# Packed half tiles in four feed-forward blocks, and a closing norm spread over more attention items, with its root taken by logarithm and exponential

## The chip, the cores and the metric

The kernel runs on one core of one Trainium2 chip, in one launch. The metric is the time of that launch on the device, in microseconds (us). The engines are TensorE (PE, whose weight loads are shown as PEld), VectorE (DVE), ScalarE (ACT), GpSimd (POOL) and SyncE (SP, which issues most loads).

## The reference

Two stacks of two layers each follow one another on 256 positions of width 1024, in float32.

The first stack works on 272 positions (16 meta positions ahead of the 256). Each layer is a SwiGLU block, a mixer (pooling, convolution, retention) and a second SwiGLU block, each closed by a residual layer norm:

```python
D_FF = ((8 * D_MODEL // 3 + 63) // 64) * 64        # 2752 = 21.5 tiles of 128

def swiglu_ffn(x, w13, w2):
    a, u = jnp.split(x @ w13, 2, axis=-1)
    return (jax.nn.silu(a) * u) @ w2
```

So there are four such blocks, and their hidden width is 21 tiles of 128 and one half tile of 64. The second stack is a diffusion-style transformer. Its first layer has a mixer of two parts, neighbourhood attention (8 heads of 64) and a bidirectional mLSTM (4 heads of 128), and the mLSTM's output is closed per head:

```python
def _mlstm_output(h, o_pre, g):
    h = sigmoid(o_pre) * h
    mu = jnp.mean(h, axis=-1, keepdims=True)
    var = jnp.mean(jnp.square(h - mu), axis=-1, keepdims=True)
    h = (h - mu) * lax.rsqrt(var + EPS)
    return h * g
```

Both parts go side by side through one output projection.

## The kernel before

All activations are kept feature-major: 128 features on the partitions, positions along the free axis. Each float32 weight is split into a high part, rounded to fp32r, and the rest, and so is each activation. A product of the two is three matmuls into the same PSUM tile: high by high, high by low, low by high (`three`, all of them recorded at line 448, where `mm` stands).

**Weights.** They come in units of 1 MB, a tile of 128 partitions by 2048 floats, each 16 blocks of 128 by 128. SP loads them in order into four slots (`load_unit`, L462). A load waits until the matmuls that read the slot's last unit are done. ACT makes the high part (`high`, L1430), DVE the rest (`rest`, L1975), and `w1_split` tells PE that a unit is ready.

**A feed-forward block of the first stack** (`ffn1`) has 33 units: 22 up units (f = 0 to 21), each with one tile of the gate and one of the value, 48 matmuls in all, and 11 down units (d = 0 to 10), two hidden tiles each, also 48 matmuls. The half tile (f = 21) is padded with zeros to a whole one in both. For each f, ACT takes the silu of the gate's tile from PSUM (L1487), DVE multiplies the value's tile on it (`gate`, L2118), ACT rounds it (`gate_high`, L1491), and DVE takes the rest (`gate_low`, L2122). DVE's program has the order `gate(step - 1)`, `rest` of the unit two ahead, some operations of the modulation's product (`ada_ops`, L2003 and L2006), `gate_low(step - 1)`. How many of those operations a step takes is said by `ada_due`: 3 in most up steps, 2 in every fourth, 4 in nine of the down steps, 96 in all. After steps 10, 15 and 21 DVE takes a finished part of the modulation from PSUM bank 7 (`ada_take`, L2011). The down product begins with the eight output tiles in the order 6, 2, 3, 4, 5, 7, 0, 1 (bank j holds tile j); tile 7 waits for that `ada_take`, tile 0 for the last `gate`. The last two down units are done tile by tile, so that tiles are finished one after another. Six DVE additions and the norm follow.

**The attention of the second stack's first layer** runs 32 items (`attend` on PE and DVE, `softmax` on ACT), items 0 to 15 over 256 keys and 16 to 31 over 512. For item n PE's program has the scores of n + 2 (and a bias product from item 16 on), the transposes of n (L1188), the values of n - 1, and then `between(n)`. DVE has the row maximum, the sum's reciprocal, the scaling of the probabilities, the placing of the output, and `between(n)`; ACT the exponential, two copies, and `between(n)`. `between` is where the mLSTM's closing norm is fitted in, by `head_norm(n - HEAD_SHIFT)`, with `HEAD_SHIFT` 14:

- items 12 to 15: for each head a mean by a product with ones (PE), the centring (DVE, L2504), the square (ACT, L1793)
- item 16: the variances of all four heads, into 32 partitions each (PE); item 17: the square root (ACT, L1796, into the tile `HSTD`); item 18: its reciprocal (DVE, L2507)
- items 18 to 21: for each head a product that spreads the reciprocals over all partitions (PE); items 19 to 22 the gain (DVE, L2511); items 20 to 24 the rounding and the rest (ACT L1799, DVE L2516)

The squares and `HSTD` lie in the weights' fourth slot, so SP waits for the last of those spreading products (`head_mm`) before it loads the unit `E_WOUT + 3`, one of the output projection's.

Of the kernel before, what the change touches and what calls it, by code (L numbers as in the profile page):

```python
# [71 lines left out]
def build(nc, A, out):  # L72
    with ExitStack() as ctx:
# [214 lines left out]
        GATES_OUT, CUM_OUT, NF_OUT = 1, 2, 3  # L288
        WG_SPLIT, GATES_ABS, LS_MIN, LS_DONE, CUM_COPIED, ROWS_COPIED, NF_COPIED = 1, 4, 5, 6, 7, 8, 9
        WG_HIGH, GATES_EXP, GATES_LN = 1, 2, 3  # L290
        HEAD_VAR, HEAD_STD = 5, 5
        HEAD_SHIFT = 14
        OG_TAKEN, VM_TAKEN = 6, 8
        OD_DQ, OD_CK, OD_KPE, OD_QR = 1, 2, 3, 4

# [11 lines left out]
        def conv_at(i, f):  # L307
            return 8 + FT * i + f + 1

        HEAD_CENTRED, HEAD_RSTD = (1, 2, 3, 4), 5  # L310
        HEAD_Y, HEAD_LOW = (6, 7, 8, 10), (9, 11, 12, 13)


        w1_loaded = [sem(f"w1_loaded{s}") for s in range(SLOTS)]
# [105 lines left out]

        ADA_FROM = [0]
# [246 lines left out]
        def _(pe):  # L668
# [5 lines left out]
            def three(o, n, b, hi, lo, first, last):  # L674
# [81 lines left out]
            def ffn1(l, b):  # L756
# [34 lines left out]
                for j in range(CT):  # L791
                    for d in range(DN_EARLY, DN_UNITS):
                        for kk in range(2):
                            k = 2 * d + kk
                            last = three(PS[:, j, tk], u0 + FT + d, kk * CT + j, GHI[:, k, tk], GLO[:, k, tk], False,
                                         k == FT - 1)
# [345 lines left out]
            def head_norm(n):  # L1142


                if n in (-2, -1, 0, 1):
                    h = n + 2
                    if h < 2:
                        pe.wait_ge(na_taken, NA_TILES)
                    else:
                        pe.wait_ge(head_step, HEAD_CENTRED[h - 2])  # L1150
                    pe.wait_ge(ml_out, h + 1)
                    mm(pe, PS[:, h % 2, :], ONES[:, 2, :], G[:, 8 + h, :], True, True).then_inc(head_mm, 1)
                elif n == 2:
                    pe.wait_ge(head_step, HEAD_CENTRED[3])
                    pe.wait_ge(pool2_step, ROW_SET)
                    for h in range(MLH):
                        pe.wait_ge(head_act, h + 1)
                        last = mm(pe, PS[32 * h:32 * h + 32, 0, :], ONES[:, 2, 0:32], OSQ2[:, h, :], True, True)
                    last.then_inc(head_mm, 1)
                elif n in (4, 5, 6, 7):  # L1160
                    h = n - 4
                    pe.wait_ge(head_step, HEAD_RSTD)
                    if h >= 2:
                        pe.wait_ge(head_step, HEAD_Y[h - 2])
                    mm(pe, PS[:, (h + 1) % 2, :], ROW2[32 * h:32 * h + 1, :], HSTD[32 * h:32 * h + 1, :], True, True)\
                        .then_inc(head_mm, 1)
# [250 lines left out]
        def _(act):  # L1417
# [3 lines left out]
            def high(n):  # L1421
# [8 lines left out]
                act.copy(WHI1[:, s, :], RAW[:, s, :]).then_inc(w1_high, 1)  # L1430

            def norm_out(e, gain, bias):
                tk = tokens(e - 1)
# [43 lines left out]
            def ffn1(l, b):  # L1477
# [4 lines left out]
                def silu(f):  # L1482
                    n, value = released[u0 + f]
                    act.wait_ge(n, value)
                    if FT * i + f >= 2:
                        act.wait_ge(g_low, FT * i + f - 1)
                    act.activation(SG[:, f % 2, tk], PS[:, 2 * (f % 3), tk], ACT.Silu).then_inc(silu1_done, 1)  # L1487

                def gate_high(f):
                    act.wait_ge(gated, FT * i + f + 1)  # L1490
                    act.copy(GHI[:, f, tk], SG[:, f % 2, tk]).then_inc(g_high, 1)  # L1491

                high(u0 + 2)
                high(u0 + 3)
# [292 lines left out]

            def head_norm(n):

                if n in (0, 1, 2):  # L1790
                    for h in ((0, 1), (2,), (3,))[n]:
                        act.wait_ge(head_step, HEAD_CENTRED[h])
                        act.activation(OSQ2[:, h, :], G[:, 8 + h, :], ACT.Square).then_inc(head_act, 1)  # L1793
                elif n == 3:
                    act.wait_ge(head_mm, HEAD_VAR)
                    act.activation(HSTD[:, :], PS[:, 0, :], ACT.Sqrt, bias=EPS6[:, 0:1]).then_inc(head_act, 1)  # L1796
                elif n in (6, 7, 8, 9):
                    act.wait_ge(head_step, HEAD_Y[n - 6])
                    act.copy(XB[:, :, 0, 4 + n - 6, :], two(G[:, 8 + n - 6, :])).then_inc(head_act, 1)  # L1799

            def softmax(items, base, probs, turned, banks, between):
                def copy_turned(n):
# [163 lines left out]
        def _(v):  # L1966
            v.memset(MODF[:, :, :], 0.0).then_inc(start_set, 1)

            def rest(n):

                if n >= UNITS:
                    return
                s = slot_of[n]
                v.wait_ge(w1_high, highs[n])
                v.tensor_tensor(WLO1[:, s, :], RAW[:, s, :], WHI1[:, s, :].bitcast(F32), ALU.subtract)\  # L1975
                    .then_inc(w1_split, 1)

            gst = Steps(v, gains_step)
# [131 lines left out]
            def ffn1(l, b):  # L2110
# [3 lines left out]

                def gate(f):
                    v.wait_ge(silu1_done, FT * i + f + 1)
                    t = SG[:, f % 2, tk]
                    v.tensor_tensor(t, t, PS[:, 2 * (f % 3) + 1, tk], ALU.mult).then_inc(gated, 1)  # L2118

                def gate_low(f):  # L2120
                    v.wait_ge(g_high, FT * i + f + 1)
                    v.tensor_tensor(GLO[:, f, tk], SG[:, f % 2, tk], GHI[:, f, tk].bitcast(F32), ALU.subtract)\  # L2122
                        .then_inc(g_low, 1)

                rest(u0 + 2)
# [372 lines left out]

            def head_norm(n):

                if n in (-2, -1, 0, 1):
                    h = n + 2
# [5 lines left out]
                if 5 <= n < 5 + MLH:  # L2508
                    h = n - 5
# [3 lines left out]
                if 7 <= n < 7 + MLH:  # L2513
                    h = n - 7
# [183 lines left out]
def up_units(w):  # L2698

    h = w.shape[1] // 2  # L2700
    w = np.pad(w.reshape(D, 2, h), ((0, 0), (0, 0), (0, FF - h)))
    return w.reshape(CT, P, 2, FT, P).transpose(3, 1, 2, 0, 4).reshape(FT, P, 2 * D)


def down_pairs(w):

    w = np.pad(w, ((0, FF - w.shape[0]), (0, 0)))
    return w.reshape(DN_UNITS, 2, P, CT, P).transpose(0, 2, 1, 3, 4).reshape(DN_UNITS, P, 2 * D)


# [137 lines left out]
```

## Time and profile before

| | |
|---|---|
| median of 3 runs | 2326.58 us (2322.51 to 2329.9) |
| the profiled execution | 2322.65 us, its span 2320.9 us |
| PE busy in the span | 2216.4 us (96%) |
| PEld | 2030.0 us (87%) |
| DVE | 1611.2 us (69%) |
| ACT | 1046.7 us (45%) |
| POOL | 209.8 us (9%) |
| mean granted TensorE clock | 0.969 |
| HBM | 330.5 MB read, 143 GB/s |

The profile is that of one execution. Its own time is 3.9 us under the median and equal to the fastest of the three runs. A matmul's duration in it is longer than the time that it adds, since matmuls overlap: what one costs is read from the start of one to the start of the next, or from the number of them in a stretch that PE fills. A bracket at the end of a timeline's line gives the idle time of the engine just ahead of it and whom it waited for.

### The profile page before, as it was taken

The page shows a single profiled execution, that of the slowest core. Times are in us where ns is not written, and L with a number is a line of the kernel's source. Part 1 is how long each engine was busy: PE and PEld are TensorE (multiplying, and loading weights), DVE is VectorE, ACT ScalarE, POOL GpSimd, SP SyncE. Part 2 cuts the span into 40 slices and gives each one's busy share as a digit, 9 for nine tenths or more (in the row PEclk, how much of TensorE's full clock was granted, in tenths as well). Part 3 has the DMA queues.
Part 4 walks back from the last instruction along what each step waited for, and adds up shares of the span by engine and source line. Part 5 has one row for each costly group of instructions (what it writes and reads, how often), then busy time and mean ns, then how long its engine had stood idle before and what let it go on. Part 6 is the DMA issues. An engine that isn't in the chain of part 4 may idle for free. (4 is left out here: it accounts for less than half of the span.)

```text
span 2320.9 us, 35981 instructions
## 1 busy us (share of the span) xinstructions
PE 2216.4 (96%) x15136; PEld 2030.0 (87%) x15136; DVE 1611.2 (69%) x2407; ACT 1046.7 (45%) x1512; POOL 209.8 (9%) x219
## 2 busy tenths in 40 slices
PE   6999998999999999899999998999999997997997
PEld 6999978999999997899999776698888886687997
DVE  5878886877887789697853467666455437757774
ACT  5433535433544344444444335534444323755662
POOL 2100232100210023210100001000000000100000
PEclk9999989999999999999998999999999998998998
DMA  5665524667466552476522112022322222113552
GB/s 212 241 218 204 193 73 152 241 224 255 182 220 218 199 193 85 186 256 236 201 91 79 55 55 79 19 73 91 105 95 91 104 78 74 54 42 115 186 177 100
DMA packets 47488, 333.86 MB, mean 144 GB/s; under 512 B 5532, under 2 KB 6652, under 8 KB 7776
## 3 DMA queue, kind: packets, MB, share of 16 engines
q1 hardware_dynamic: 37808, 268.45, 32.3%
q0 software_dynamic: 9520, 63.11, 7.3%
q8 instruction: 120, 1.97, 0.3%
q14 instruction: 40, 0.33, 0.0%
HBM read 330.50 MB, written 1.05 MB: 143 GB/s over the span
## 5 line engine op out<-in xcount | busy, mean ns | idle before, releaser
L1975 DVE TENSOR_TENSOR WLO<-RAW,WHI 128x2048 fp32r<-128x2048 f32 x252 | 587.9, 2335 | 269.4 <-ACT WHI L1430 266.6
L448 PE MATMUL PS<-XB,WHI 128*128 128x256 f32 (+1 forms) x3072 | 701.0, 323 | 15.5 <-DVE XB L2320 10.7
L1430 ACT CAST WHI<-RAW 128x2048 fp32r<-128x2048 f32 x252 | 479.8, 1907 | 317.8 <-DMA RAW<-in_dn_c 79.8
L448 PEld LDWEIGHTS PS<-XB,WHI 128*128 128x128 f32 x3072 | 517.4, 192 | 62.8 <-issue 18.1
L448 PE MATMUL PS<-XHI,WHI 128*128 128x272 f32 (+1 forms) x1792 | 523.3, 295 | 18.3 <-ACT XHI L1438 14.9
L448 PE MATMUL PS<-XHI,WLO 128*128 128x272 f32 (+1 forms) x1792 | 518.1, 292 | 0.0
L448 PE MATMUL PS<-XLO,WHI 128*128 128x272 f32 (+1 forms) x1792 | 495.2, 290 | 0.0
L448 PE MATMUL PS<-XB,WLO 128*128 128x256 f32 (+1 forms) x1536 | 494.0, 322 | 0.0
L448 PEld LDWEIGHTS PS<-XHI,WHI 128*128 128x128 f32 x1792 | 346.3, 193 | 23.8 <-issue 18.8
L448 PEld LDWEIGHTS PS<-XHI,WLO 128*128 128x128 f32 x1792 | 345.8, 193 | 0.0
L448 PEld LDWEIGHTS PS<-XLO,WHI 128*128 128x128 f32 x1792 | 334.1, 192 | 0.4
L448 PEld LDWEIGHTS PS<-XB,WLO 128*128 128x128 f32 x1536 | 294.9, 192 | 21.1
L2006 DVE SCALAR_TENSOR_TENSOR AP<-AW,SC,AP 128x512 f32<-128x512 f32 x336 | 241.5, 770 | 0.0
L448 PE MATMUL PS<-GHI,WLO 128*128 128x272 f32 (+1 forms) x704 | 201.3, 286 | 0.0
L448 PE MATMUL PS<-GHI,WHI 128*128 128x272 f32 (+1 forms) x704 | 201.2, 286 | 0.0
L448 PE MATMUL PS<-GLO,WHI 128*128 128x272 f32 (+1 forms) x704 | 201.0, 285 | 0.0
L2364 DVE SCALAR_TENSOR_TENSOR AC<-CB,FCW,AC 128x512 f32<-128x512 f32 (+1 forms) x176 | 97.1, 614 | 134.0 <-ACT AC L1658 103.8
L1487 ACT ACTIVATE SG<-PS 128x272 f32<-128x272 f32 (+1 forms) x88 | 34.2, 394 | 224.4 <-PE PS L448 224.4
L448 PEld LDWEIGHTS PS<-GHI,WHI 128*128 128x128 f32 x704 | 132.5, 188 | 0.0
L448 PEld LDWEIGHTS PS<-GHI,WLO 128*128 128x128 f32 x704 | 132.4, 188 | 0.0
L448 PEld LDWEIGHTS PS<-GLO,WHI 128*128 128x128 f32 x704 | 132.4, 188 | 0.0
L1656 ACT COPY CB<-PS 128x512 f32<-128x512 f32 x52 | 27.9, 589 | 114.0 <-PE PS L448 114.0
(362 smaller groups left out, 2735.1 us busy)
## 6 DMA issues: line engine op xcount, KB each, us to landing
AW<-in_ada POOLq DMA_DIRECT2D x48, 1024.0 KB, 6.7
RAW<-in_up_a SPq DMA_DIRECT2D x44, 1024.0 KB, 4.9
RAW<-in_up_b SPq DMA_DIRECT2D x44, 1024.0 KB, 4.9
RAW<-in_up_c SPq DMA_DIRECT2D x44, 1024.0 KB, 4.9
RAW<-in_mix SPq DMA_DIRECT2D x30, 1024.0 KB, 4.9
RAW<-in_dn_a SPq DMA_DIRECT2D x22, 1024.0 KB, 4.9
RAW<-in_dn_b SPq DMA_DIRECT2D x22, 1024.0 KB, 4.9
RAW<-in_dn_c SPq DMA_DIRECT2D x22, 1024.0 KB, 4.8
```

The costliest lines, as they stand in the source:

```text
L448: return pe.matmul(o, w, x, start=first, stop=last)
L1430: act.copy(WHI1[:, s, :], RAW[:, s, :]).then_inc(w1_high, 1)
L1487: act.activation(SG[:, f % 2, tk], PS[:, 2 * (f % 3), tk], ACT.Silu).then_inc(silu1_done, 1)
L1656: act.copy(cb[:, a, :, 1:257], two(PS[:, banks + a, :]))
L1975: v.tensor_tensor(WLO1[:, s, :], RAW[:, s, :], WHI1[:, s, :].bitcast(F32), ALU.subtract)\
L2006: v.scalar_tensor_tensor(a, w, c, a, ALU.mult, ALU.add).then_inc(ada_step, 1)
L2364: return v.scalar_tensor_tensor(o, i, vec(a, t), o, ALU.mult, ALU.add)
```

## The change

1. **Half tiles, up product.** The last up unit of each of the four blocks holds 64 columns of the gate and 64 of the value in one tile. It is 1024 floats wide: half of it is loaded, rounded and split, and PE does 24 matmuls in place of 48. Silu reads the lower 64 partitions, `gate` the upper 64 as the other operand.
2. **Half tiles, down product.** The hidden tile 21 holds its high part on the lower 64 partitions and its low part on the upper 64; the weights' rows are there twice. Two matmuls over 128 rows (`stacked`) take the place of three, eight output tiles in each block.
3. **`ada_due`**: the last up step takes no modulation operations in place of 3, steps 3 and 7 take 3 in place of 2, the sum stays 96.
4. **The closing norm** runs from item 10 to item 28: means at items 10, 11, 13, 14, each centring one item later and each square two; variances at item 18; at item 19 a logarithm, at item 20 an exponential of minus half of it (both ACT) in place of the square root and the reciprocal; spreading products at items 21, 22, 24, 25, the gain one item later, the rounding two, the rest three.

```diff
-        HEAD_VAR, HEAD_STD = 5, 5
-        HEAD_SHIFT = 14
+        HEAD_VAR, HEAD_LN, HEAD_STD = 5, 5, 6
+        HEAD_SHIFT = 10
+        MEAN_AT, SPREAD_AT = (0, 1, 3, 4), (11, 12, 14, 15)
...
+        HALF_UNITS = tuple(u + FT - 1 for u in (0, UNITS_B0, UNITS_LAYER, UNITS_LAYER + UNITS_B0))
+
+        def width(n):
+
+            return D if n in HALF_UNITS else 2 * D
+
+        def rows_of(f, a=0):
+
+            return slice(0, P) if f < FT - 1 else slice(64 * a, 64 * a + 64)
...
-                return 2 if step % 4 == 3 else 3 if step < FT else 0
+                return 0 if step == FT - 1 else 2 if step in (11, 15, 19) else 3
...
-                sp.dma_start(RAW[:, slot_of[n], :], src).then_inc(w1_loaded[slot_of[n]], 16)
+                w = width(n)
+                sp.dma_start(RAW[:, slot_of[n], 0:w], src[:, 0:w]).then_inc(w1_loaded[slot_of[n]], 16)
...
+            def stacked(o, n, b, hl, first, last):
+
+
+                wh, wl = block_of(n, b)
+                mm(pe, o, wh, hl, first, False)
+                return mm(pe, o, wl, hl, False, last)
...
-                for j in range(2):
+                for j in range(width(n) // D):
...
+                            if k == FT - 1:
+                                last = stacked(PS[:, j, tk], u0 + FT + d, kk * CT + j, GHI[:, k, tk], False, True)
...
-                elif n == 2:
+                elif n == 8:
...
-                elif n in (4, 5, 6, 7):
-                    h = n - 4
-                    pe.wait_ge(head_step, HEAD_RSTD)
+                elif n in SPREAD_AT:
+                    h = SPREAD_AT.index(n)
+                    pe.wait_ge(head_act, HEAD_STD)
...
-                elif n == 3:
+                if n == 9:
                     act.wait_ge(head_mm, HEAD_VAR)
-                    act.activation(HSTD[:, :], PS[:, 0, :], ACT.Sqrt, bias=EPS6[:, 0:1]).then_inc(head_act, 1)
+                    act.activation(HSTD[:, :], PS[:, 0, :], ACT.Ln, bias=EPS6[:, 0:1]).then_inc(head_act, 1)
+                if n == 10:
+                    act.wait_ge(head_act, HEAD_LN)
+                    act.activation(HSTD[:, :], HSTD[:, :], ACT.Exp, scale=-0.5).then_inc(head_act, 1)
...
-                    t = SG[:, f % 2, tk]
-                    v.tensor_tensor(t, t, PS[:, 2 * (f % 3) + 1, tk], ALU.mult).then_inc(gated, 1)
+                    t = SG[rows_of(f), f % 2, tk]
+                    u = PS[rows_of(f, 1), 2 * (f % 3) + (f < FT - 1), tk]
+                    v.tensor_tensor(t, t, u, ALU.mult).then_inc(gated, 1)
...
+                    r = rows_of(f)
+                    o = GLO[:, f, tk] if f < FT - 1 else GHI[rows_of(f, 1), f, tk]
+                    v.tensor_tensor(o, SG[r, f % 2, tk], GHI[r, f, tk].bitcast(F32), ALU.subtract)\
...
-                if n in (-2, -1, 0, 1):
-                    h = n + 2
+                if n - 1 in MEAN_AT:
+                    h = MEAN_AT.index(n - 1)
...
-                if n == 4:
-                    v.wait_ge(head_act, HEAD_STD)
-                    v.reciprocal(HSTD[:, :], HSTD[:, :]).then_inc(head_step, 1)
```

## Rows read from the trace of the kernel before

**Rows 1.** The page, part 1: busy time of each engine.

```profile
PE 2216.4 (96%) x15136; PEld 2030.0 (87%) x15136; DVE 1611.2 (69%) x2407; ACT 1046.7 (45%) x1512; POOL 209.8 (9%) x219
```

**Rows 2.** Windows: us, busy PE, PEld, DVE, ACT, POOL, granted clock, DMA share, GB/s.

```profile
42.00:170.00 128.00, 127.89 (x1016) 127.51 (x1015) 105.34 (x124) 51.88 (x63) 12.72 (x12) 1.00 0.64 230
977.00:1097.00 120.00, 119.65 (x1011) 119.35 (x1010) 103.56 (x134) 51.15 (x62) 12.21 (x12) 1.00 0.71 255
```

**Rows 3.** Timeline of ACT, end of the first block's up half.

```profile
170.45 0.40 ACT L1487 ACTIVATE SG<-PS 128x272 f32<-128x272 f32 x1 [3.55 <-PE PS L448]
171.27 1.91 ACT L1430 CAST WHI<-RAW 128x2048 fp32r<-128x2048 f32 x1 [0.42 <-DMA RAW<-in_dn_a]
```

**Rows 4.** Timeline of DVE, the same place.

```profile
166.62 2.29 DVE L1975 TENSOR_TENSOR WLO<-RAW,WHI 128x2048 fp32r<-128x2048 f32 x1 [1.36 <-ACT WHI L1430]
168.83 2.07 DVE L2006 SCALAR_TENSOR_TENSOR AP<-AW,SC,AP 128x512 f32<-128x512 f32 x3
170.82 0.43 DVE L2122 TENSOR_TENSOR GLO<-SG,GHI 128x272 fp32r<-128x272 f32 x1
171.17 0.16 DVE L2011 TENSOR_TENSOR MOD<-PS,ADAB 128x8 f32<-128x8 f32 x1
```

**Rows 5.** Timeline of ACT, fourth feed-forward block.

```profile
1017.95 0.38 ACT L1487 ACTIVATE SG<-PS 128x256 f32<-128x256 f32 x1
...
1097.13 0.39 ACT L1487 ACTIVATE SG<-PS 128x256 f32<-128x256 f32 x1 [3.20 <-PE PS L448]
```

**Rows 6.** Timeline of DVE, fourth feed-forward block.

```profile
1013.19 2.28 DVE L1975 TENSOR_TENSOR WLO<-RAW,WHI 128x2048 fp32r<-128x2048 f32 x1
...
1093.66 2.29 DVE L1975 TENSOR_TENSOR WLO<-RAW,WHI 128x2048 fp32r<-128x2048 f32 x1 [1.38 <-ACT WHI L1430]
```

**Rows 7.** Timeline of PE, the first attention.

```profile
1431.14 0.44 PE L1188 MATMUL PS<-IDN,PR 128*128 128x128 f32 x2 [0.32 <-DVE PR L2534]
...
1434.08 0.44 PE L1188 MATMUL PS<-IDN,PR 128*128 128x128 f32 x2 [0.32 <-DVE PR L2534]
...
1437.07 0.44 PE L1188 MATMUL PS<-IDN,PR 128*128 128x128 f32 x2 [0.81 <-DVE PR L2534]
...
1437.79 1.02 PE L448 MATMUL PS<-G,ONES 128*128 128x512 f32 x2
1438.65 1.02 PE L448 MATMUL PS<-G,QZ 128*128 128x512 f32 x2
...
1451.96 1.10 PE L448 MATMUL PS<-G,QZ 128*128 128x512 f32 x2 [0.89 <-ACT PR L1821]
...
1457.91 1.12 PE L448 MATMUL PS<-HSTD,ROW 1*128 1x512 f32 x2 [3.09 <-DVE HSTD L2507]
...
1465.90 0.60 PE L1188 MATMUL PS<-IDN,PR 128*128 128x128 f32 x4
...
1469.77 0.60 PE L1188 MATMUL PS<-IDN,PR 128*128 128x128 f32 x4
...
1482.11 0.60 PE L1188 MATMUL PS<-IDN,PR 128*128 128x128 f32 x4
...
1484.74 0.60 PE L1188 MATMUL PS<-IDN,PR 128*128 128x128 f32 x4
```

**Rows 8.** Timeline of ACT, the square root in the attention.

```profile
1447.75 1.28 ACT L1796 ACT_TABLE_LOAD   x1
...
1449.75 1.28 ACT L1821 ACT_TABLE_LOAD   x1
```

**Rows 9.** Timeline of DVE, the reciprocal of the roots.

```profile
1454.53 3.33 DVE L2507 RECIPROCAL HSTD<-HSTD 128x512 f32<-128x512 f32 x1
```

**Rows 10.** Window behind that wait, columns as in rows 2.

```profile
1458.00:1462.50 4.50, 4.50 (x11) 2.42 (x12) 0.97 (x2) 0.00 (x0) 0.00 (x0) 0.62 0.00 0
```

**Rows 11.** Timeline of ACT, table loads around the gates' logarithm.

```profile
1265.23 1.28 ACT L1734 ACT_TABLE_LOAD   x1
...
1304.45 1.28 ACT L1775 ACT_TABLE_LOAD   x1
```

More of the change, by code:

```diff
@@ L308, in conv_at @@
             return 8 + FT * i + f + 1
-        HEAD_CENTRED, HEAD_RSTD = (1, 2, 3, 4), 5
-        HEAD_Y, HEAD_LOW = (6, 7, 8, 10), (9, 11, 12, 13)
+        HEAD_CENTRED = (1, 2, 3, 4)
+        HEAD_Y, HEAD_LOW = (5, 6, 8, 10), (7, 9, 11, 12)
         w1_loaded = [sem(f"w1_loaded{s}") for s in range(SLOTS)]
@@ L794, in ffn1 @@
                             k = 2 * d + kk
-                            last = three(PS[:, j, tk], u0 + FT + d, kk * CT + j, GHI[:, k, tk], GLO[:, k, tk], False,
-                                         k == FT - 1)
+                            if k == FT - 1:
+                                last = stacked(PS[:, j, tk], u0 + FT + d, kk * CT + j, GHI[:, k, tk], False, True)
+                            else:
+                                last = three(PS[:, j, tk], u0 + FT + d, kk * CT + j, GHI[:, k, tk], GLO[:, k, tk],
+                                             False, False)
                     last.then_inc(tile_out, 1)
@@ L1142, in head_norm @@
             def head_norm(n):
-                if n in (-2, -1, 0, 1):
-                    h = n + 2
+                if n in MEAN_AT:
+                    h = MEAN_AT.index(n)
                     if h < 2:
@@ L1429, in high @@
                     act.wait_ge(r, value)
-                act.copy(WHI1[:, s, :], RAW[:, s, :]).then_inc(w1_high, 1)
+                w = width(n)
+                act.copy(WHI1[:, s, 0:w], RAW[:, s, 0:w]).then_inc(w1_high, 1)
             def norm_out(e, gain, bias):
@@ L1486, in silu @@
                         act.wait_ge(g_low, FT * i + f - 1)
-                    act.activation(SG[:, f % 2, tk], PS[:, 2 * (f % 3), tk], ACT.Silu).then_inc(silu1_done, 1)
+                    r = rows_of(f)
+                    act.activation(SG[r, f % 2, tk], PS[r, 2 * (f % 3), tk], ACT.Silu).then_inc(silu1_done, 1)
                 def gate_high(f):
                     act.wait_ge(gated, FT * i + f + 1)
-                    act.copy(GHI[:, f, tk], SG[:, f % 2, tk]).then_inc(g_high, 1)
+                    r = rows_of(f)
+                    act.copy(GHI[r, f, tk], SG[r, f % 2, tk]).then_inc(g_high, 1)
                 high(u0 + 2)
@@ L1788, in head_norm @@
             def head_norm(n):
[L1790 to L1793, printed above, removed]
-                elif n == 3:
-                    act.wait_ge(head_mm, HEAD_VAR)
-                    act.activation(HSTD[:, :], PS[:, 0, :], ACT.Sqrt, bias=EPS6[:, 0:1]).then_inc(head_act, 1)
-                elif n in (6, 7, 8, 9):
-                    act.wait_ge(head_step, HEAD_Y[n - 6])
-                    act.copy(XB[:, :, 0, 4 + n - 6, :], two(G[:, 8 + n - 6, :])).then_inc(head_act, 1)
+                if n - 2 in MEAN_AT:
+                    h = MEAN_AT.index(n - 2)
+                    act.wait_ge(head_step, HEAD_CENTRED[h])
+                    act.activation(OSQ2[:, h, :], G[:, 8 + h, :], ACT.Square).then_inc(head_act, 1)
+                if n == 9:
+                    act.wait_ge(head_mm, HEAD_VAR)
+                    act.activation(HSTD[:, :], PS[:, 0, :], ACT.Ln, bias=EPS6[:, 0:1]).then_inc(head_act, 1)
+                if n == 10:
+                    act.wait_ge(head_act, HEAD_LN)
+                    act.activation(HSTD[:, :], HSTD[:, :], ACT.Exp, scale=-0.5).then_inc(head_act, 1)
+                if n - 2 in SPREAD_AT:
+                    h = SPREAD_AT.index(n - 2)
+                    act.wait_ge(head_step, HEAD_Y[h])
+                    act.copy(XB[:, :, 0, 4 + h, :], two(G[:, 8 + h, :])).then_inc(head_act, 1)
             def softmax(items, base, probs, turned, banks, between):
@@ L1974, in rest @@
                 v.wait_ge(w1_high, highs[n])
-                v.tensor_tensor(WLO1[:, s, :], RAW[:, s, :], WHI1[:, s, :].bitcast(F32), ALU.subtract)\
+                w = width(n)
+                v.tensor_tensor(WLO1[:, s, 0:w], RAW[:, s, 0:w], WHI1[:, s, 0:w].bitcast(F32), ALU.subtract)\
                     .then_inc(w1_split, 1)
@@ L2499, in head_norm @@
             def head_norm(n):
-                if n in (-2, -1, 0, 1):
-                    h = n + 2
+                if n - 1 in MEAN_AT:
+                    h = MEAN_AT.index(n - 1)
                     v.wait_ge(head_mm, h + 1)
                     v.tensor_tensor(G[:, 8 + h, :], G[:, 8 + h, :], PS[:, h % 2, :], ALU.subtract).then_inc(head_step, 1)
-                if n == 4:
-                    v.wait_ge(head_act, HEAD_STD)
-                    v.reciprocal(HSTD[:, :], HSTD[:, :]).then_inc(head_step, 1)
-                if 5 <= n < 5 + MLH:
-                    h = n - 5
+                if n - 1 in SPREAD_AT:
+                    h = SPREAD_AT.index(n - 1)
                     v.wait_ge(head_mm, HEAD_VAR + h + 1)
@@ L2512, in head_norm @@
                                            ALU.mult, ALU.mult).then_inc(head_step, 1)
-                if 7 <= n < 7 + MLH:
-                    h = n - 7
+                if n - 3 in SPREAD_AT:
+                    h = SPREAD_AT.index(n - 3)
                     v.wait_ge(head_act, HEAD_STD + h + 1)
@@ L2700, in up_units @@
     h = w.shape[1] // 2
-    w = np.pad(w.reshape(D, 2, h), ((0, 0), (0, 0), (0, FF - h)))
-    return w.reshape(CT, P, 2, FT, P).transpose(3, 1, 2, 0, 4).reshape(FT, P, 2 * D)
+    if h == FF:
+        return w.reshape(CT, P, 2, FT, P).transpose(3, 1, 2, 0, 4).reshape(FT, P, 2 * D)
+    w = w.reshape(CT, P, 2, h)
+    full = w[:, :, :, 0:FF - P].reshape(CT, P, 2, FT - 1, P).transpose(3, 1, 2, 0, 4).reshape(FT - 1, P, 2 * D)
+    half = w[:, :, :, FF - P:h].transpose(1, 0, 2, 3).reshape(1, P, D)
+    return np.concatenate([full, np.pad(half, ((0, 0), (0, 0), (0, D)))], 0)
 def down_pairs(w):
-    w = np.pad(w, ((0, FF - w.shape[0]), (0, 0)))
+    w = np.concatenate([w, w[FF - P:]], 0) if w.shape[0] < FF else w
     return w.reshape(DN_UNITS, 2, P, CT, P).transpose(0, 2, 1, 3, 4).reshape(DN_UNITS, P, 2 * D)
```

2 lines of the change are left out of this document (1 added, 1 removed).

## The prediction

> **What bounds the kernel now.** I read the page first. Part 1 has the matmuls busy nearly all the time and every other engine well below [rows 1], so what counts is work on PE and the places where PE waits. Busy time is an average, so the next view is the windows of the two stages that the change touches. In the first feed-forward block the 128.00 us from 42 to 170 hold 1016 matmuls at full clock with PE busy 127.89 us; in the fourth block, with 256 columns in place of 272, 120.00 us hold 1011 [rows 2]. PE is the bound there, and a matmul costs 128.00/1016 = 0.126 us in the first three blocks and 120.00/1011 = 0.119 us in the fourth. DVE is the next in line: 105 of 128 us, and 104 of 120.
>
> The attention is another case. I read PE's timeline by its transposes, one group for each item, since the distance from one group to the next is the pace of an item [rows 7]. Items 10 and 11 take (1434.08 - 1431.14)/2 = 1.47 us each, and PE waits 0.32 us for DVE ahead of the transposes of items 10 and 12: a chain over three engines sets this pace, not PE. Item 25 takes 1484.74 - 1482.11 = 2.63 us with PE full. From item 10's transposes to item 26's it is 53.60 us, and this is where the closing norm lies. The longest wait in it is PE's 3.09 us for the reciprocal, which itself runs 3.33 us on DVE [rows 7, 9]. In the window that follows the granted clock is 0.62 over 4.50 us [rows 10], a stretch partly at the lower of its two levels, right behind a stretch in which PE did nothing; it costs 4.50 x 0.38 = 1.7 us more.
>
> **Part 1: half tiles.** Each block loses 24 matmuls of the last up unit and 8 of the last down unit. Both stand on PE, the bound: 3 blocks x 32 x 0.126 = 12.1 us and 32 x 0.119 = 3.8 us, together 15.9 us. Rounding, rest and load of that unit are halved as well; that is worth nothing, as ACT and DVE have gaps there (DVE waited 1.36 us for ACT ahead of a rest) [rows 4].
>
> What may be given back lies at the seam between the last up unit and the down product. In the first block silu of f = 21 starts at 170.45 [rows 3], when its unit ends, so the unit before ended at 170.45 - 48 x 0.126 = 164.40. After the change the last unit ends at 164.40 + 24 x 0.126 = 167.42, and PE reaches output tile 7 after 15 more matmuls, at 169.31. Tile 7 waits for the modulation's take on DVE. DVE's order is the rest from 166.62, then the three modulation operations from 168.83, `gate_low`, the take [rows 4]. The three operations have left that step, so `gate_low` starts at 168.83, the take 0.35 us behind it and ends 0.16 us later, at 169.34: PE waits about 0.1 us. The last `gate`, 0.43 us from about 169.26, is done at 169.69, which is when PE comes to tile 0 (18 matmuls, 169.69). In the fourth block the same sum from 1097.13 [rows 5] gives an up unit ending at 1091.42, the half one at 1094.28, tile 7 due at 1096.06; the rest begins at 1093.66 [rows 6], so the take ends at 1093.66 + 2.21 + 0.35 + 0.16 = 1096.38, 0.3 us late, 0.4 with the semaphore. I take 3 x 0.1 + 0.4 = 0.7 us off: 15.2 us. Bounds: nothing is given back (15.9), or DVE comes a whole rest too late in each block (4 x 2.3 = 9.2, leaving 6.7). I stay near the first, because the order of instructions is fixed and the rows that I shifted are the same instructions.
>
> The three modulation operations go to other steps: one to step 3, one to step 7, one drops into the sum of the later steps. One costs 2.07/3 = 0.69 us [rows 4]. Their cover is DVE's lead over PE, smallest in the fourth block: the rest of unit 9 starts at 1013.19 and is done at 1015.5, and PE needs it when silu of f = 8 starts, 1017.95 [rows 5, 6]. That is 2.4 us of cover for the one operation that lies ahead of it. Cost: nothing; without the cover it would be 0.7 us for each of 8.
>
> The loads behind: unit 24 landed at 171.27, 6.9 us after the slot was free at 164.40, then 1.91 us of rounding and 2.29 us of rest, ready at 175.5 [rows 3, 4]. PE wants it two down units (12.1 us) after the last up unit, before at 182.5, now at 179.5. The cover shrinks from 7.0 to 4.0 us. Cost: nothing.
>
> **Part 2: the norm.** I add up the pace of items 10 to 25 after the change. A mean takes 1438.65 - 1437.79 = 0.86 us of PE [rows 7]. In the short items 10 and 11 some 0.3 us of it falls into PE's own gap and the chain may take more, so 0.56 to 0.86, say 0.7: 2 x 2.2 = 4.4. Item 12 has a centring on DVE and a square on ACT but no mean: between 1.47 and the 2.99 us of a short item with mean and centring in one (1434.08 to 1437.07) [rows 7]; I take 1.9, since DVE no longer waits for PE within an item. Items 13 and 14 have a mean again beside 512-key scores, 3.0 each as that row. Items 15 and 16: 3.0 less the mean, 2.1, and 0.2 for DVE and ACT: 4.6. Item 17: 2.6. Item 18 has the variances; their price is taken as that of a spreading product, whose item took 1469.77 - 1465.90 = 3.87 us, 1.24 over the plain pace: 3.8. Item 19 has the logarithm. Before, ACT's block of table load, root and second table load [rows 8] made PE wait 0.89 us for the next exponential [rows 7]; the logarithm stands in the same order behind the variances, so the wait returns: 2.63 + 0.9 + 0.2 = 3.7. Item 20 has the exponential on HSTD, an ACT instruction like the softmax's own, with no load: 2.7, as ACT is far from full. Items 21, 22, 24, 25 have the spreads, 4 x 3.87 = 15.5; item 23 is 2.7. The sum is 4.4 + 1.9 + 6.0 + 4.6 + 2.6 + 3.8 + 3.7 + 2.7 + 15.5 + 2.7 = 47.9 us against 53.6: 5.7 us gained. It agrees with what leaves: 3.1 us of wait and 1.7 us of lower clock, and 0.8 us at each of two short items, 6.4, less small slips. Bounds: 7.5 if the chain takes nothing beyond PE's work; 0.4 if each of the short and middle items goes at the 2.99 of before.
>
> SP's wait: the load of the unit `E_WOUT + 3` now starts behind item 25's spread, four items later. Items 26 to 31 at 2.63 us leave 15.8 us, the load takes 6.9 at the pace above, and ACT rounds it only after the last item. Nothing behind it on SP can start before the output projection frees a slot. Cost: nothing.
>
> **Do logarithm and exponential share a table?** The trace has the same pair in the gates' step: a table load ahead of the logarithm at 1265.23 and another at 1304.45 ahead of the next exponential, with copies alone between [rows 11]. So the two functions are in different tables here, and the change keeps two loads where the root had two. The Trainium skill (ScalarE: Activation LUTs, "Table sets: the hidden batching unit") says that one set holds both, so that this pair needs one load. The trace disagrees. By that rule the block at item 19 would shrink to the logarithm alone.
>
> **Sum.** 15.2 + 5.7 = 20.9 us. Against the profiled execution's 2322.65 us that is 2301.7. This execution lay 3.9 us under the median of the three runs, and from the median the same sum gives 2305.7. I say 2304. A measurement of this kernel can tell about 0.3% (7 us) from no change.
>
> **Rivals.**
> - Tables are shared: PE's 0.9 us wait at item 19 and its 0.2 go, total 22.0, 2303. Against it: rows 11. Chance 6%.
> - The chain over three engines eats the norm's gain: 15.2 + 0.4 = 15.6, 2309. For it: PE already waits for DVE in the short items. Against it: each step now has an item's time. 8%.
> - DVE is a rest too late at the seam in all four blocks: 6.7 + 5.7 = 12.4, 2312. Against it: it asks for a rounding 2.3 us later than rows 4 have. 8%.
> - Both of these and a little more, under 7 us in all: 2322. 4%.
> - Slower: late weights. Loads are asked for 3 us sooner while the modulation's are in flight, and the cover is 4.0 us. If they landed more than 6.9 + 4.0 = 10.9 us after the slot is free, PE would wait in the down half; at 1 us for each of 40 down units it is 40 - 20.9 = 19 us slower, 2342. Up to 10.9 us it costs nothing. 3%.
> - More than 24 us gained, by something that I don't see: 2299. 5%.
>
> The forecast itself has the remaining 66%, and its own range is 2299 to 2309. The range for 8 in 10 is 2297 to 2312; it takes in both readings of the base and the second and most of the third rival. Faster by over 0.3%: 66 + 6 + 8 + 8 + 5 = 93%; within it 4%; slower 3%.
>
> **What would show it.** In each block the last two silus 3.0 us apart (2.8 in the fourth) and PE full through the seam; two matmuls in place of three for hidden tile 21; 128 matmuls fewer. In the attention no reciprocal of 128 by 512 on DVE, no wait of PE over 1.2 us, the clock at full, two table loads around the logarithm, and some 48 us from item 10's transposes to item 26's. The prediction is wrong if PE waits at tile 7 for more than 1 us, if ACT waits long for down units, or if the short items go on at 3 us.

## The result and the profile after

The changed kernel took 2306.15 us in the median of five runs (2299.75 to 2310.17), the kernel before 2322.51 us in the five beside them (2318.57 to 2329.9). The ratio is 0.9917, with a 95% interval of 0.9898 to 0.9936: 19.3 us less, 14.9 to 23.7 (the two medians by themselves lie 16.4 us apart). In a second comparison it was 0.9927 (0.9905 to 0.9948), with the medians 16.0 us apart. The forecast was 2304 us, with 2297 to 2312 for 8 in 10.

The profiled execution is the fastest of the five: 2299.75 us, span 2297.9 us, 22.9 less than its counterpart. Part 1 of its page answers to [rows 1], 128 matmuls fewer as counted:

```profile
PE 2194.2 (95%) x15008; PEld 2007.0 (87%) x15008; DVE 1605.1 (70%) x2406; ACT 1041.6 (45%) x1513; POOL 210.4 (9%) x219
```

**The seam.** The timelines of ACT, DVE and PE's weight loads in the first block, which answer to [rows 3, 4]:

```profile
164.64 0.40 ACT L1511 ACTIVATE SG<-PS 128x272 f32<-128x272 f32 x1 [5.34 <-PE PS L459]
...
167.67 0.39 ACT L1511 ACTIVATE SG<-PS 64x272 f32<-64x272 f32 x1 [0.52 <-PE PS L459]
```

```profile
166.87 2.29 DVE L2005 TENSOR_TENSOR WLO<-RAW,WHI 128x2048 fp32r<-128x2048 f32 x1 [1.36 <-ACT WHI L1453]
169.08 0.43 DVE L2155 TENSOR_TENSOR GLO<-SG,GHI 128x272 fp32r<-128x272 f32 x1
169.43 0.16 DVE L2041 TENSOR_TENSOR MOD<-PS,ADAB 128x8 f32<-128x8 f32 x1
169.62 0.44 DVE L2149 TENSOR_TENSOR SG<-SG,PS 64x272 f32<-64x272 f32 x1
```

```profile
167.34 0.19 PEld L459 LDWEIGHTS PS<-GHI,WHI 128*128 128x128 f32 x1
...
169.64 0.19 PEld L459 LDWEIGHTS PS<-GHI,WHI 128*128 128x128 f32 x1 [0.35 <-DVE MOD L2041]
169.75 0.19 PEld L459 LDWEIGHTS PS<-GLO,WHI 128*128 128x128 f32 x1
169.88 0.19 PEld L459 LDWEIGHTS PS<-GHI,WLO 128*128 128x128 f32 x1
170.11 0.19 PEld L459 LDWEIGHTS PS<-GHI,WHI 128*128 128x128 f32 x1
```

The last two silus are 3.03 us apart. PE begins the down product at 167.34, 0.33 us before the last silu starts, so tile 7 is due at 167.34 + 15 x 0.126 = 169.23, and the take on DVE is over at 169.59. PE goes on at 169.64, 0.4 us late, and three matmuls later it stands again, now for tile 0 and the last `gate`, for 0.1 us.

A good yardstick for a block is the time from the silu of f = 20 to the first row of the closing norm on DVE (the subtraction that makes the variance), since neither end depends on what lies before the block. Before it is 74.92 us in each of the first three blocks and 70.73 in the fourth; after, 71.51, 71.51, 71.50 and 67.82. That is 13.15 us in four blocks.

**The attention.** PE's timeline, to be held against [rows 7]; the times are the starts of items 10, 18, 19, 20, 25 and 26, the wait stands in item 19:

```profile
1412.86 0.44 PE L1210 MATMUL PS<-IDN,PR 128*128 128x128 f32 x2 [0.32 <-DVE PR L2564]
...
1432.33 0.60 PE L1210 MATMUL PS<-IDN,PR 128*128 128x128 f32 x4
...
1436.14 0.60 PE L1210 MATMUL PS<-IDN,PR 128*128 128x128 f32 x4
...
1438.36 1.10 PE L459 MATMUL PS<-G,QZ 128*128 128x512 f32 x2 [0.72 <-ACT PR L1850]
...
1439.72 0.60 PE L1210 MATMUL PS<-IDN,PR 128*128 128x128 f32 x4
...
1456.84 0.60 PE L1210 MATMUL PS<-IDN,PR 128*128 128x128 f32 x4
...
1460.71 0.60 PE L1210 MATMUL PS<-IDN,PR 128*128 128x128 f32 x4
```

Item 10 to item 26 takes 1460.71 - 1412.86 = 47.85 us against 53.60. The 3.09 us wait is gone. ACT's timeline at item 19, and the window of the attention (columns as in rows 2):

```profile
1434.14 1.28 ACT L1821 ACT_TABLE_LOAD   x1
1435.43 0.69 ACT L1821 ACTIVATE HSTD<-PS,EPS 128x512 f32<-128x512 f32 x1
1436.14 1.28 ACT L1850 ACT_TABLE_LOAD   x1
...
1438.73 0.64 ACT L1824 ACTIVATE HSTD<-HSTD 128x512 f32<-128x512 f32 x1
```

```profile
1412.00:1474.00 62.00, 59.03 (x324) 40.72 (x324) 41.19 (x119) 39.66 (x100) 0.00 (x0) 1.00 0.05 18
```

Two table loads stand around the logarithm as around the root in [rows 8], and the clock is full.

**The rest of the difference.** 13.15 + 5.75 = 18.9 us are at the two places of the change, near the ratio's 19.3 and inside both intervals. The spans differ by 22.9: in stretches whose instructions are the same there are 5.1 us less up to item 10 and 1.1 more after item 26. The last section shows what such differences are.

### The profile page after: what moved, and what is told of

Read it like the earlier page. It is cut to its first block and busy times, and to the rows that moved or that the text cites. A ratio compares the mean times of both kernels' runs of the same rounds, so it can differ in the third digit from the quotient of the medians.

```text
span 2297.9 us, 35725 instructions
## 1 busy us (share of the span) xinstructions
PE 2194.2 (95%) x15008; PEld 2007.0 (87%) x15008; DVE 1605.1 (70%) x2406; ACT 1041.6 (45%) x1513; POOL 210.4 (9%) x219
## 5 line engine op out<-in xcount | busy, mean ns | idle before, releaser
L459 PE MATMUL PS<-XB,WHI 128*128 128x256 f32 (+1 forms) x3072 | 701.5, 324 | 16.7 <-DVE XB L2353 12.4
L459 PE MATMUL PS<-XHI,WHI 128*128 128x272 f32 (+1 forms) x1760 | 513.4, 294 | 18.7 <-ACT XHI L1461 15.1
L459 PE MATMUL PS<-XHI,WLO 128*128 128x272 f32 (+1 forms) x1760 | 508.2, 291 | 0.0
L459 PE MATMUL PS<-XLO,WHI 128*128 128x272 f32 (+1 forms) x1760 | 486.1, 290 | 0.0
L459 PEld LDWEIGHTS PS<-XHI,WHI 128*128 128x128 f32 x1760 | 339.5, 193 | 24.2 <-issue 18.9
L459 PEld LDWEIGHTS PS<-XHI,WLO 128*128 128x128 f32 x1760 | 339.1, 193 | 0.0
L459 PEld LDWEIGHTS PS<-XLO,WHI 128*128 128x128 f32 x1760 | 328.2, 192 | 0.4
L459 PE MATMUL PS<-GLO,WHI 128*128 128x272 f32 (+1 forms) x672 | 191.8, 285 | 0.0
L459 PEld LDWEIGHTS PS<-GLO,WHI 128*128 128x128 f32 x672 | 126.5, 188 | 0.0
```

The costliest lines, as they stand in the source:

```text
L459: return pe.matmul(o, w, x, start=first, stop=last)
```

## The experiments

All comparisons are with the kernel before on the same chip; "block" is the yardstick above. Medians are in us, intervals are 95%.

**1 and 2. Each part alone.** The edits are the hunks of the diff for the half tiles and for the norm.

> The four blocks with packed half tiles, the closing norm as before. Theory A (gains are local and add up): from the silu of f = 20 to the norm's variance row each block is as short as in the changed kernel (71.5 us in the first three, 67.8 in the fourth, against 74.9 and 70.7), 13.2 us in all; the attention keeps its 53.6 us from item 10 to item 26; ratio to the kernel before 0.994. Theory B (the shorter blocks also speed up what follows, as the first mixer was 4.0 us shorter in the one profile of the changed kernel): the stages between the blocks are shorter too, 17 to 20 us in all, ratio 0.992.

Measured: 2310.69, ratio 0.9942 (0.9924 to 0.996), 13.5 us. Blocks 71.51, 73.72, 71.50, 67.96. The three stretches between the blocks, each from a variance row to the next block's first silu, are not shorter: 344.9 us together, 344.3 before (the first mixer 164.92 and 164.20). So theory A, but for the second block: the four blocks give 10.8 us here. The second block is 2.2 us long because of one late load. ACT's, DVE's and PE's rows of it:

```profile
577.86 1.91 ACT L1452 CAST WHI<-RAW 128x2048 fp32r<-128x2048 f32 x1 [8.42 <-DMA RAW<-in_dn_b]
```

```profile
579.81 2.29 DVE L2000 TENSOR_TENSOR WLO<-RAW,WHI 128x2048 fp32r<-128x2048 f32 x1 [5.39 <-ACT WHI L1452]
```

```profile
582.15 0.39 PE L458 MATMUL PS<-GHI,WHI 128*128 128x272 f32 x1 [1.48 <-DVE WLO L2000]
```

It is the block's last down unit. ACT waited 8.42 us for it, where its waits for the six down units before it are 3.7 to 4.6. In the profile before, ACT waits 7.49 us for the down unit four places earlier in this block, and PE does not wait. The load itself was slow: SP asked for it at 568.71, and it landed 9.1 us later, where the block's other down units take 4.8 to 5.6 us. POOL's queue had asked for a 1 MB load of the modulation's weights at 568.70, and that one took 9.3.

> Only the closing norm is spread and its root taken by logarithm and exponential; the blocks are as before. Theory A: item 10 to item 26 takes 47.9 us in place of 53.6, nothing else moves, ratio 0.9975. Theory B (part of the 22.9 us between the two profiles was not from either edit's place): the blocks and mixers differ from those of the kernel before by as much as 4 us either way although no instruction of theirs is changed, and the ratio still says 0.9975 within its interval.

Measured: 2321.08, ratio 0.9982 (0.9972 to 0.9992), 4.2 us; item 10 to item 26 takes 47.85 us; blocks as before to 0.01 us. Theory A holds, and so does what B says of the other stretches: its first mixer takes 159.44 us, 4.8 less than before, with the same instructions. The ratios of the two parts add up to 17.7 us.

**3 to 6. The seam.**

```diff
 for step in range(3, FT + 1):
-    gate(step - 1)
+    if step < FT:
+        gate(step - 1)
+    if step == FT - 1:
+        ada_take(6 * i + 2, 1, 6 * i + 3)
     rest(u0 + step + 2)
     ada_ops(i, step)
+    if step == FT - 1:
+        gate(step)
     gate_low(step - 1)
...
-    if step in (10, 15, 21):
-        n = (10, 15, 21).index(step)
+    if step in (10, 15):
+        n = (10, 15).index(step)
```

> The changed kernel, with DVE's order at the seam changed: the modulation's take goes ahead of the rest of the unit two ahead, and the last gate goes ahead of the low part of f = 20. Theory A (what the blocks fall short of 32 matmuls is mostly PE's wait at tile 7 and tile 0): PE waits for no DVE work at the seam, the stretch from the silu of f = 20 to the variance row falls from 71.5 to 71.0 us in three blocks and from 67.8 to 67.1 in the fourth, 2.2 us in all, 2304. Theory B (the shortfall is at the block's end, where the last two output tiles come faster than DVE and POOL add them up): the stretch stays at 71.5 and 67.8.

Measured: 2300.89, ratio 0.9894 (0.9879 to 0.991). Blocks 71.09, 72.56, 71.09, 67.42. Theory A in the first and the third block. The second had again a late last down unit (PE's weight loads waited 1.0 us for its rest). The fourth missed its 67.1: PE's weight loads still wait there 0.29 us for the last `gate`, which DVE can begin only when it has done the rest of the unit two ahead, at 1080.6. DVE's order in the second profile of this kernel, where the take is done 3.6 us before PE wants it and the last `gate` when PE gets to it:

```profile
165.35 0.16 DVE L2041 TENSOR_TENSOR MOD<-PS,ADAB 128x8 f32<-128x8 f32 x1
166.79 2.29 DVE L2005 TENSOR_TENSOR WLO<-RAW,WHI 128x2048 fp32r<-128x2048 f32 x1 [1.28 <-ACT WHI L1453]
169.11 0.44 DVE L2149 TENSOR_TENSOR SG<-SG,PS 64x272 f32<-64x272 f32 x1
169.47 0.43 DVE L2155 TENSOR_TENSOR GLO<-SG,GHI 128x272 fp32r<-128x272 f32 x1
```

The take alone moved:

> The changed kernel with the modulation's take alone moved ahead of the rest; the last gate stays behind the low part of f = 20. Theory A (tile 0's wait for the last gate stands right behind tile 7's for the take): PE no longer waits at tile 7, but about 0.3 us at tile 0, since the gate is only 0.16 us sooner; from the silu of f = 20 to the variance row 71.35 us, where both moves gave 71.09 and neither 71.51. Theory B (tile 7's wait is the only one): 71.09.

Measured: 2305.48 (one run); blocks 71.42, 71.56, 71.43, 67.76. PE's weight loads at tile 0:

```profile
169.54 0.19 PEld L459 LDWEIGHTS PS<-GHI,WHI 128*128 128x128 f32 x1 [0.36 <-DVE SG L2149]
```

Theory A: the wait passed from the take to the gate, and in the first block 0.09 of 0.42 us was won.

The old `ada_due`, put back into the changed kernel:

```diff
-                return 0 if step == FT - 1 else 2 if step in (11, 15, 19) else 3
+                return 2 if step % 4 == 3 else 3
```

> The changed kernel with the modulation's operations dealt out as before: three again in the last up step, two in steps 3 and 7. Theory A (DVE is the late one at the seam, so every us put ahead of the take counts in full): PE's wait at tile 7 grows from 0.4 to 2.5 us in each block, the stretch from the silu of f = 20 to the variance row is 73.6 us (69.9 in the fourth), 8.3 us slower than the changed kernel, 2314. Theory B (PE has other work ahead of tile 7 that covers it): under 0.5 us per block, within 2 us of the changed kernel.

Measured: 2312.51, ratio 0.9943 (0.9922 to 0.9964). Blocks 73.49, 73.50, 73.49, 71.38. The waits of PE's weight loads up to 1180 us (total, times, longest) are, in this kernel and then in the changed one:

```profile
PEld PS L459 <- DVE MOD L2041: 9.6, 4, 2.6
```

```profile
PEld PS L459 <- DVE MOD L2041: 1.6, 4, 0.6
```

Theory A: 8.0 us more of waiting. So leaving these operations at the seam would have cost more than the norm's whole edit gains. The fourth block lost 1.5 us beyond its 2.0 us of wait. Behind the wait, of 2.38 us for PE's matmuls there, the granted clock was at its lower level; behind the waits of the other three blocks, 2.1 us each, it was 1.00 over the like 3.2 us:

```profile
1095.80:1099.00 3.20, 3.20 (x15) 3.20 (x16) 1.71 (x2) 2.73 (x3) 0.00 (x0) 0.50 0.46 195
```

15 matmuls are done in a time in which 27 fit at 0.119 us each: 12 x 0.119 = 1.4 us.

**7. The down product alone.** The last up unit padded and done with 48 matmuls again, `gate` reading its second tile.

> The changed kernel with the last up unit padded to whole tiles again (48 matmuls, 2048 floats wide), the down product still with two matmuls for hidden tile 21. Theory A (the seam loses only because the half unit brings PE there 3.0 us sooner): no wait at tile 7, and of the 8 matmuls saved 6 lie ahead of the block's last DVE burst, so from the silu of f = 20 to the variance row it is 74.1 us (70.0 in the fourth) against 74.9 and 70.7 of before and 71.5 and 67.8 of the changed kernel, 10 us slower than the changed kernel, 2316. Theory B (part of the down saving is lost in waits for weights, which a faster down half meets): 74.5 us or more.

Measured: 2309.85, ratio 0.9932 (0.9914 to 0.9951). Blocks 74.06, 74.06, 74.05, 69.89. Theory A: the blocks came within 0.1 us of it, and PE waits nowhere for the take. 8 matmuls are worth 0.86 us, not 1.01. Most of the 0.15 is at the block's end, where PE waits for POOL's addition to the last sum: from the weight load before to the one that waited it is 0.54 us, where it was 0.42. The whole time was 6 us better than the theory had, and that is not placed: the profiled execution is the slowest of the four (2314.14), its first mixer took 162.06 us.

**8 to 10. The norm's two halves.** The root by square root and reciprocal (DVE, item 20), at the spread items:

```diff
 if n == 9:
     act.wait_ge(head_mm, HEAD_VAR)
-    act.activation(HSTD[:, :], PS[:, 0, :], ACT.Ln, bias=EPS6[:, 0:1]).then_inc(head_act, 1)
-if n == 10:
-    act.wait_ge(head_act, HEAD_LN)
-    act.activation(HSTD[:, :], HSTD[:, :], ACT.Exp, scale=-0.5).then_inc(head_act, 1)
+    act.activation(HSTD[:, :], PS[:, 0, :], ACT.Sqrt, bias=EPS6[:, 0:1]).then_inc(head_act, 1)
...
+if n == 10:
+    v.wait_ge(head_act, HEAD_STD)
+    v.reciprocal(HSTD[:, :], HSTD[:, :]).then_inc(head_step, 1)
```

> The changed kernel with its closing norm spread over the same items, but with the square root and the 3.33 us reciprocal of before in place of logarithm and exponential. Theory A (each of the two halves of the norm's edit has its own gain): DVE has about 1 us free in an item of 2.63 us, so PE waits some 2 us for it at items 20 and 21, item 10 to item 26 takes 49.9 us in place of 47.85, 2308. Theory B (the spreading alone gives it all, since the reciprocal now has an item's time): 48.2 us or less, no wait of PE over 0.5 us behind the reciprocal, within the scatter of the changed kernel.

Measured: 2312.19, ratio 0.9938 (0.9921 to 0.9955). Item 10 to 26: 50.42 us; item 20 takes 5.13 in place of 2.63. PE's row there, and the window behind it:

```profile
1459.00 0.66 PE L1210 MATMUL PS<-IDN,PR 128*128 128x128 f32 x4 [2.34 <-DVE PR L2564]
```

```profile
1459.00:1463.00 4.00, 4.00 (x19) 2.54 (x20) 1.64 (x5) 1.52 (x4) 0.00 (x0) 1.00 0.00 0
```

Then the items of before, with logarithm and exponential in one block on ACT at item 17:

> Packed half tiles as in the changed kernel, the closing norm at the items of before, but its root by logarithm and exponential, one right behind the other on ACT at item 17. Theory A: the 3.1 us wait for the reciprocal and the 1.6 to 3.3 us of lower clock behind it go, ACT's block is 0.64 us longer, items 12 to 15 keep their 3.0 us each: item 10 to item 26 takes 49.4 us, 1.5 us more than in the changed kernel, 2307. Theory B (what counts is the spreading): 52 us or more. By either theory two table loads stand around the logarithm, one of them between it and the exponential; if the two functions shared a table that one would be missing and the time 1.3 us less.

Measured: 2308.33, ratio 0.992 (0.989 to 0.9951). Item 10 to 26: 49.26 us, items 12 to 14 at 2.98 to 2.99 each. ACT's timeline, and PE's wait for it:

```profile
1438.24 1.28 ACT L1820 ACT_TABLE_LOAD   x1
1439.54 0.69 ACT L1820 ACTIVATE HSTD<-PS,EPS 128x512 f32<-128x512 f32 x1
1440.24 1.28 ACT L1822 ACT_TABLE_LOAD   x1
1441.54 0.63 ACT L1822 ACTIVATE HSTD<-HSTD 128x512 f32<-128x512 f32 x1
1442.07 0.67 ACT L1847 ACTIVATE PR<-PS,STAT 128x512 f32<-128x512 f32 x1
```

```profile
1442.98 1.10 PE L458 MATMUL PS<-G,QZ 128*128 128x512 f32 x2 [1.40 <-ACT PR L1847]
```

Theory A in both. From 53.60, the root's form alone gives 4.3 us, the spreading alone 3.2, both 5.75: they overlap, since the reciprocal's stall is in both. Item 18, in which PE waits for it, takes 8.36 us before and 3.87 with the root's form alone; where the items are only spread, the stall shrinks to the 2.5 us of item 20. The table load between logarithm and exponential settles the tables: two loads for this pair here.

> The changed kernel with one more logarithm of a single element on ACT at item 17, which is thrown away, so that two more table loads stand in an item that has no part of the norm on ACT. Theory A (ACT's block of loads at item 19 is what makes that item 1.0 us longer than a plain one): about 2.6 us more on ACT at item 17, PE waits 0.5 to 0.9 us there for the next probabilities, item 10 to item 26 takes 48.6 us in place of 47.85. Theory B (item 19 is long for its place behind the variances, and ACT has room for two loads): no change, under 0.2 us.

Measured: 2305.10 (one run). Item 17 takes 4.43 us in place of 2.62, item 10 to 26 takes 49.67. The mechanism is A's, its price twice what I gave: 2.76 us of ACT cost PE a wait of 1.58 and 1.8 us in all.

```profile
1438.65 1.10 PE L459 MATMUL PS<-G,QZ 128*128 128x512 f32 x2 [1.58 <-ACT PR L1852]
```

At item 19 the loads and the logarithm, 3.3 us, cost only 1.0. By the rows, item 18 before it has PE busy with the variances for 1.0 us more, while ACT has nothing of the norm to do; that this is the reason was not tried.

**11. Against each other.** The changed kernel and the one with take and last gate ahead, beside each other.

> The changed kernel again. The places of the change give 13.15 + 5.75 = 18.9 us in the profile: ratio 0.992. The stretches between the blocks, which the change does not touch, differ from the first profile of it by up to 4 us.

> The same kernel as in the run with the take and the last gate ahead, beside the changed kernel on one chip. Theory A: 1.7 us less than the changed kernel from the waits at the seam (0.42 in each of three blocks, 0.40 to 0.55 in the fourth), which the ratios to before can hardly tell apart. Theory B (the 5 us between the two medians so far are real): 4 us or more less than the changed kernel, and the profile shows it at another place.

Measured: 2307.89, ratio 0.9927 (0.9905 to 0.9948), and 2300.77, ratio 0.99 (0.9877 to 0.9924). Blocks of the first 71.50, 71.50, 71.51, 68.02, 13.0 us less than before, and 47.85 us from item 10 to item 26; blocks of the second 71.09, 71.09, 71.08, 67.58. So the second has the lowest median here, 7 us below the changed kernel's beside it and 5 us below in the first pair, whose two kernels were measured in different comparisons; its own places explain 1.5. The rest is not placed: in both its profiles the first mixer takes 159.5 us, in the changed kernel's two 160.2 and 166.3, but that one differs by as much between executions of one kernel. The profiled executions with the short mixer are 2299.40 and 2300.52 us in this kernel and 2299.75 in the changed one. The intervals overlap, so the size stays open.

## Why the prediction came out

It was right in both mechanisms; the sum was 2 us too large. That the median came within about 2 us of 2304 is partly luck: the base was a choice between two readings 4 us apart, the medians of the kernel before lie between 2322.51 and 2326.83 in the four comparisons, and single runs of the changed kernel between 2299.75 and 2311.28.

- **Count and price of the matmuls** (15.9 us): 128 fewer. With the seam mended the first block gains 3.83 of the 4.03 us counted, the down part alone 0.86 of 1.01. Of the missing 0.15 to 0.2 us, 0.12 is PE's longer wait for POOL at the block's end, where I had no term. The fourth block, at 3.31 of 3.81, misses 0.3 more at the last `gate`.
- **The seam** (0.7 us): the step that was mis-sized. The block keeps 15.9 - 13.15 = 2.75 us less than counted. DVE's order came to 0.01 us as shifted: the take ended 4.95 us after the silu of f = 20, forecast 4.94. PE came sooner: I took the start of the last silu for the end of its unit, and PE had left it 0.33 us earlier. I also let the last `gate` end exactly when PE came and gave it no price. DVE is 0.4 us late for either; one wait covers most of the other, and only moving both instructions won the 0.42 us.
- **The operations moved out of the seam** (nothing elsewhere, 0.7 for each where cover fails): 2.0 us of wait per block when they come back, 2.07 forecast, and in the fourth block 1.4 us of lower clock besides. At the steps that took them over they cost nothing, as forecast: from the silu of f = 5 to that of f = 20 it is 96.16 us (90.54 in the fourth block) before and after.
- **Loads behind the seam** (cost nothing, cover 4.0 us): true of unit 24. What I missed is the cover of the last down unit, 1.7 us in the second block before (rest done at 583.5, PE there at 585.2). In three of the ten profiles with half up units one late load fell on it and cost 1.5 to 2.2 us; in the three with full ones none did. The cause is not the 3 us by which PE is ahead: from SP's asking for the unit to PE's need of it there are 12.1 us before (573.1 to 585.2) and 11.7 with the half tiles alone (568.7 to 580.4). Those three loads took 8.4 to 9.1 us to land, and from there to the end of the rest it is 4.3 us more, too long in either kernel. In the other ten profiles the load took 4.9 to 7.3 us. Whether the change makes such late landings more frequent, three in ten against none in three, is not settled. The slower rival's mechanism exists, but once in a run, not at 40 units.
- **The norm** (5.7 us): 5.75. By items the forecast was within 0.2 us but for item 15, 2.77 against 2.3. Item 19, the wait for the table block, 3.58 against 3.7; the spreads 3.86 to 3.92 against 3.87. The gain is 7.4 us against the execution in which the low clock behind the reciprocal lasted longer (55.23 us, below).
- **SP's wait for the last spread** (cost nothing): true. From PE's first matmul of the output projection to the third rest that DVE starts behind it are 39.5 us before and after, and PE has the same four waits, 1.2, 0.7, 0.7 and 0.6 us, in the 210 us from the last items on.
- **The tables**: as [rows 11] said, two loads. The rival in which they are shared falls. The Trainium skill (ScalarE: Activation LUTs, "Table sets: the hidden batching unit") has one load for a logarithm and an exponential; this program's trace does not agree: the load at 1440.24, between a logarithm and an exponential with nothing else between, lasts 1.28 us.
- **The rivals** of the chain (15.6) and of a whole rest too late (12.4) did not come: no short item stayed at 2.99, and DVE was late by 0.4 us, not by 2.3.

## What to carry to other kernels

When work leaves the bound engine, write down when it arrives at its next waits by its own rows (its weight loads), not by the start of the consumer, and list every wait that is due within the time saved: the second wait takes over when the first is mended. What was saved at one place takes cover from the loads that were asked for ahead of it. Those behind it are asked for sooner as well and keep theirs (12.1 and 11.7 us from asking to need), but one slow load hits the unit with the least cover: look for that one, not only for the first. A table load costs what the next engine has no cover for: the same pair cost 1.8 us in a plain item and, with a logarithm more, 1.0 behind an item in which PE had more to do. And look at the granted clock behind every wait of PE: one of 2.38 us cost 1.4 us more that way, others of nearly its length nothing.

## What the runs showed of the hardware

**Waits and the clock.** Behind PE's 3.09 us wait for the reciprocal the granted clock fell, and for how long differed: in the run with the half tiles alone it was 0.57 over 8 us, and item 10 to 26 took 55.23 us; before, 0.79 over the 8 us that begin likewise. Behind waits of 2.34, 1.58 and 1.40 us in the experiments it stayed full, behind the one of 2.38 us in the fourth block with the operations at the seam it was 0.50 over 3.2 us. With 2.34 and 2.38 so near each other, these rows give no length of wait from which on the clock falls. Rows of the run with the half tiles alone, then of before:

```profile
1448.00:1456.00 8.00, 7.14 (x18) 4.23 (x18) 3.46 (x9) 0.59 (x1) 0.00 (x0) 0.57 0.01 2
```

```profile
1457.00:1465.00 8.00, 7.08 (x21) 3.93 (x22) 3.81 (x9) 1.90 (x4) 0.00 (x0) 0.79 0.00 0
```

**Why like stretches differ.** The 12 us behind the second block's variance row, the same instructions, in the profile before, after, and of the norm alone:

```profile
599.98:611.98 12.00, 12.00 (x76) 12.00 (x77) 10.33 (x17) 8.78 (x18) 0.00 (x0) 0.72 0.32 131
```

```profile
589.93:601.93 12.00, 12.00 (x89) 12.00 (x90) 10.31 (x17) 8.79 (x18) 0.00 (x0) 0.86 0.30 128
```

```profile
595.88:607.88 12.00, 12.00 (x65) 12.00 (x66) 10.32 (x17) 8.79 (x18) 0.00 (x0) 0.59 0.31 128
```

In the mixers there are two courses. In the first mixer of the norm alone the clock is at its lower level (0.50) while DVE is late, so that PE, itself slower, waits at most 0.5 us for it, and full behind it; before, PE runs at full clock, waits 2.57 us for DVE at 329.22, and has 0.57 over the next 16 us. That mixer is 4.8 us longer. Rows of before first:

```profile
329.22 5.91 PE L448 MATMUL PS<-QK 64*128 64x272 f32 x12 [2.57 <-DVE ST L2193]
```

```profile
320.00:328.00 8.00, 6.52 (x47) 5.79 (x45) 8.00 (x12) 2.60 (x4) 5.03 (x6) 1.00 0.20 55
329.00:345.00 16.00, 15.78 (x49) 10.67 (x50) 10.46 (x16) 4.52 (x5) 0.00 (x0) 0.57 0.03 13
```

```profile
320.00:328.00 8.00, 8.00 (x26) 6.03 (x26) 8.00 (x8) 3.09 (x4) 6.96 (x7) 0.50 0.00 0
331.00:347.00 16.00, 16.00 (x90) 12.32 (x89) 12.97 (x18) 8.92 (x14) 0.00 (x0) 1.00 0.19 67
```

All thirteen profiles follow one of the two. In eight PE waits 2.57 us there, with the clock at 1.00 ahead of the wait and 0.57 or 0.58 behind it, and the mixer takes 164.0 to 166.5 us; in five it does not, with 0.50 to 0.53 ahead and 0.97 to 1.00 behind, and it takes 159.4 to 162.1. The changed kernel has one profile of either kind, so the edits do not decide it; what does is open.

So one pair of profiles of this kernel can be 5 us off in stretches that nobody changed, and only yardsticks inside a stretch bound by PE repeat well: the first and the third block to 0.01 us in the profiles of the same seam, the fourth to 0.2.

**One DVE operation at two speeds.** The same fourteen tap operations of the mixer take 5.85 us and, while POOL works on its pooling, 11.90; DVE's timeline before, then POOL's:

```profile
303.85 5.85 DVE L2171 SCALAR_TENSOR_TENSOR ACC<-CP,VEC,ACC 128x272 f32<-128x272 f32 x14
...
316.28 11.90 DVE L2171 SCALAR_TENSOR_TENSOR ACC<-CP,VEC,ACC 128x272 f32<-128x272 f32 x14
```

```profile
314.26 5.90 POOL L586 TENSOR_TENSOR PT<-PT 128x570 f32<-128x570 f32 x3
320.23 3.66 POOL L590 TENSOR_TENSOR WN<-PT,IC 64x272 f32<-64x272 f32 x4
323.97 1.44 POOL L593 TENSOR_TENSOR PM<-WN,XP 128x544 f32<-128x544 f32 x1
```

Of the second fourteen, the eight that start before POOL is done at 325.41 take 1.01 to 1.60 us each, and the six that start behind it 0.49. The first fourteen, beside which POOL did nothing, take 0.48 or 0.49 each. The eight long ones make DVE late for PE at 329.22. That POOL causes it was not tried; the times coincide.
